# SSD stage: the mask is taken out of the matrix products, relu per head and one exponential over eight heads on ScalarE, inputs times step sizes as a product on VectorE

## The reference

```python
def ssd_chunked(xh, dt, A, Bm, Cm):
    x = (xh * dt[..., None]).reshape(...)
    a_cs = jnp.cumsum((dt * A).reshape(...), axis=2)
    seg = a_cs[:, :, :, None] - a_cs[:, :, None, :]
    decay = jnp.exp(jnp.where(causal, seg, -jnp.inf))
    cb = jnp.einsum('bclgn,bcsgn->bclsg', Cc, Bc)
    y_diag = jnp.einsum('bclsg,bclsgr,bcsgrp->bclgrp', cb, decay, x)
    decay_to_end = jnp.exp(a_cs[:, :, -1:] - a_cs)
    states = jnp.einsum('bclgn,bclgr,bclgrp->bcgrpn', Bc, decay_to_end, x)
    chunk_decay = jnp.exp(a_cs[:, :, -1])
    ...  # prev: the states before each chunk, from a scan over chunks
    y_off = jnp.einsum('bclgn,bcgrpn,bclgr->bclgrp', Cc, prev, jnp.exp(a_cs))
    return y_diag + y_off
```

## Time and profile before

| what | value |
|---|---|
| median of 3 runs | 1305.43 us (1304.57 to 1306.7) |
| profiled execution, its own time | 1318.41 us |
| its span | 1316.6 us |
| mean granted TensorE clock | 0.993 |
| TensorE busy, matmuls | 1268.5 us (96% of the span) |
| VectorE busy | 626.0 us (48%) |
| ScalarE busy | 386.7 us (29%) |
| GpSimd busy | 720.0 us (55%) |

### The profile page before, as it was taken

How to read it: one execution, slowest core, us unless ns; L and a number is a source line. 1 busy time by engine, 2 the same in 40 slices (tenths; PEclk the granted TensorE clock), 3 DMA queues, 4 the chain that set the end, 5 groups by cost and what they waited for, 6 DMA issues and landing times.

```text
span 1316.6 us, 19001 instructions
## 1 busy us (share of the span) xinstructions
PE 1268.5 (96%) x7442; PEld 911.3 (69%) x7442; DVE 626.0 (48%) x1035; ACT 386.7 (29%) x766; POOL 720.0 (55%) x752
## 2 busy tenths in 40 slices
PE   7999989999999999999999999999998989999997
PEld 7888768787788667888887887888887333333333
DVE  4252361448993583625854686633416322222225
ACT  5111272422333584112124644621113111111111
POOL 6677636576775302766774355665843555555430
PEclk9999999999999999999999999999999989999999
DMA  6622211432132200242222214832297599999965
GB/s 240 182 80 97 96 34 47 153 102 97 64 129 96 97 1 1 96 164 97 96 73 77 60 50 144 336 96 86 74 394 264 202 400 358 386 386 390 392 247 192
DMA packets 86845, 216.54 MB, mean 164 GB/s; under 512 B 24292, under 2 KB 33484, under 8 KB 73188
## 3 DMA queue, kind: packets, MB, share of 16 engines
q1 hardware_dynamic: 63132, 199.36, 41.2%
q0 software_dynamic: 14064, 8.45, 2.2%
q10 hardware_dynamic: 9560, 7.51, 1.9%
HBM read 252.98 MB, written 25.96 MB: 212 GB/s over the span
## 4 chain that ended last, share of the span: by engine, by line
PE 81%; DVE 7%; another core or an unknown queue 4%; ACT 2%; issue 2%; POOL 2%; DVEq 2%; DMA 0%; SPq 0%; POOLq 0%; ACTq 0%
PE ps L186 18%; PE ps L188 18%; PE ps L187 18%; PE ps L1217 10%; PE ps L1232 3%; PE ps L882 2%; POOL w_lo L1296 1%; PE ps L1095 1%; PE ps L1003 1%; PE ps L1208 1%; PE ps L1011 1%; PE ps L1087 1%; PE ps L1106 1%; DVE ps L2507 1%
## 5 line engine op out<-in xcount | busy, mean ns | idle before, releaser
L1293 POOL CAST w_hi<-stage 128x512 fp32r<-128x512 f32 (+1 forms) x280 | 179.4, 682 | 359.8 <-PE ps L188 350.0
L1296 POOL TENSOR_TENSOR w_lo<-stage,w_hi 128x512 fp32r<-128x512 f32 (+1 forms) x280 | 363.3, 1328 | 10.1
L186 PE MATMUL ps<-hi,w_hi 128*128 128x512 f32 (+1 forms) x608 | 236.9, 390 | 1.2 <-DVE lo L1890 0.6
L187 PE MATMUL ps<-hi,w_lo 128*128 128x512 f32 (+1 forms) x608 | 235.0, 386 | 0.0
L188 PE MATMUL ps<-lo,w_hi 128*128 128x512 f32 (+1 forms) x608 | 235.0, 386 | 0.0
L186 PE MATMUL ps<-w_hi,hi 128*128 128x512 f32 (+1 forms) x488 | 176.0, 361 | 1.5 <-POOL w_lo L1296 0.9
L187 PE MATMUL ps<-w_hi,lo 128*128 128x512 f32 (+1 forms) x488 | 174.7, 358 | 0.0
L188 PE MATMUL ps<-w_lo,hi 128*128 128x512 f32 (+1 forms) x488 | 174.7, 358 | 0.0
L1217 PE MATMUL ps<-w_gu,xT 128*64 128x512 f32 x736 | 166.0, 604 | 0.4 <-DVE xT L2526 0.4
L186 PEld LDWEIGHTS ps<-hi,w_hi 128*128 128x128 f32 x608 | 114.2, 188 | 27.7 <-issue 3.0
L188 PEld LDWEIGHTS ps<-lo,w_hi 128*128 128x128 f32 x608 | 114.2, 188 | 23.2
(11 more groups left out here) (489 smaller groups left out, 1763.5 us busy)
## 6 DMA issues: line engine op xcount, KB each, us to landing
stage<-w_in SPq DMA_DIRECT2D x84, 512.0 KB, 4.5
w_gu<-w_gate SPq DMA_DIRECT2D x32, 1024.0 KB, 10.0
w_gu<-w_up SPq DMA_DIRECT2D x32, 1024.0 KB, 11.9
w_dn<-w_down SPq DMA_DIRECT2D x32, 1024.0 KB, 14.4
stage<-w_out SPq DMA_DIRECT2D x16, 512.0 KB, 4.5
stage<-w_ssd_branch SPq DMA_DIRECT2D x16, 512.0 KB, 4.8
stage<-w_in SPq DMA_DIRECT2D x20, 256.0 KB, 3.1
stage<-w_attn_branch SPq DMA_DIRECT2D x8, 512.0 KB, 4.2
```

The lines of the kernel that those rows point to most:

```text
L186: pe.matmul(out, x[0], w[0], start=first, stop=False)
L187: pe.matmul(out, x[1], w[0], start=False, stop=False)
L1293: nc.gpsimd.tensor_copy(hi[:, b, k, 0:n], stage[:, b, k, 0:n])
L1296: last = nc.gpsimd.tensor_tensor(lo[:, b, k, 0:n], stage[:, b, k, 0:n], hi[:, b, k, 0:n].bitcast(F32), ALU.subtract)
```

## The change

The masks (L1066) go, with their constants, casts and loads. PSUM then holds the cumulated sum of the later token alone. Per head, ScalarE takes relu(sum of the earlier token - sum of the later one), which is zero where the later token comes first, and after eight heads one exponential of minus that, in place in `decay`. The triangle in `cb` removes what is then 1 there. dt is no longer in the exponent: VectorE multiplies the inputs with it (`xd`), TensorE's products read `xd` and wait for `xd_ready`, and `xe` is made from `xd`. The cap of `weighted` goes, so it is a plain product. `xe` shares its place with `yoff`, which takes one more drain. The waits for `acs_ready` (TensorE) and for `mT_saved` (VectorE) go too.

```diff
@@ SP
             sp.wait_ge(mT_half, 2)
-            sp.dma_start(block_of[:], d["c_block"]).then_inc(block_in, 16)
-            sp.dma_start(later[:], d["c_later"]).then_inc(block_in, 16)
             sp.dma_start(mT_dram, mT[:]).then_inc(mT_saved, 16)
@@ TensorE, spread
                 for b in range(4):
                     turns.bank(b, turns.k)
-                    rows = slice(64 * (b % 2), 64 * (b % 2 + 1))
-                    pe.matmul(ps[s][:, b, :].rearrange("p (h l) -> p h l", h=4), block_r[rows, :], bc(later_r[rows, :], 1, 4), start=True, stop=False)
...
-                                         acs_rows[rows, P * c:P * (c + 1)], start=False, stop=(j == 3))
+                                         acs_rows[rows, P * c:P * (c + 1)], start=True, stop=True)
...
-            pe.wait_ge(acs_ready, 1)
...
                 s = turns.take()
+                pe.wait_ge(xd_ready, c + 1)
...
-                        last = pe.matmul(ps[s][l, h // 8, HD * (h % 8):HD * (h % 8 + 1)], decay[:, h, l], xtok[:, c, HD * h:HD * (h + 1)],
+                        last = pe.matmul(ps[s][l, h // 8, HD * (h % 8):HD * (h % 8 + 1)], decay[:, h, l], xd[:, h, :],
@@ ScalarE
-                    A.wait_ge(dt_step, 3)
-                    A.activation(dt_log[:], dts[:, 2], ACT.Ln).then_inc(dt_act, 1)
...
-            A.activation(acs[:, 2], acs[:, 0], ACT.Exp, scale=-1.0)
+            A.activation(acs[:, 2], acs[:, 0], ACT.Exp)
...
-                        last = A.activation(decay[:, hh, :], ps[s][:, h // 4, P * (h % 4):P * (h % 4 + 1)], ACT.Exp,
-                                            bias=from_bias[:, c, hh:hh + 1])
+                        last = A.activation(decay[:, hh, :], ps[s][:, h // 4, P * (h % 4):P * (h % 4 + 1)], ACT.Relu,
+                                            scale=-1.0, bias=acs[:, 0, c, hh:hh + 1])
                         if h % 8 == 7:
-                            last.then_inc(e_ready, 1)
                             A.drain().then_inc(turn_free[s], 1)
+                            some = decay[:, hh - 7:hh + 1, :]
+                            A.activation(some, some, ACT.Exp, scale=-1.0).then_inc(e_ready, 1)
@@ VectorE
-            V.tensor_scalar(dts[:, 2], dts[:, 0], 1e-37, None, ALU.max)
...
-            V.tensor_scalar(acs[:, 0], sums[:, :, 0, :], -1.0, None, ALU.mult)
+            V.tensor_copy(acs[:, 0], sums[:, :, 0, :])
...
-            V.wait_ge(dt_act, 3)
-            V.tensor_tensor(from_bias[:], dt_log[:], acs[:, 0], ALU.add)
-            V.drain()
-            V.tensor_tensor(acs[:, 1], acs[:, 3], from_bias[:], ALU.add)
-            V.wait_ge(mT_saved, 16)
-            V.wait_ge(block_in, 32)
-            V.tensor_copy(later_r[:], later[:])
-            V.tensor_copy(block_r[:], block_of[:])
+            V.tensor_tensor(acs[:, 1], acs[:, 3], acs[:, 0], ALU.subtract)
...
-                    V.scalar_tensor_tensor(m, m, 3e38, bc(cb[:, g, :], 1, 8), ALU.min, ALU.mult).then_inc(m_ready, 1)
+                    V.tensor_tensor(m, m, bc(cb[:, g, :], 1, 8), ALU.mult).then_inc(m_ready, 1)
...
                 V.tensor_tensor(skip[:], heads(c), bc(d_skip[:], 2, HD), ALU.mult)
+                V.tensor_tensor(xd[:], heads(c), bc(dts[:, 0, c, :], 2, HD), ALU.mult).then_inc(xd_ready, 1)
...
                     V.tensor_tensor(skip[:], skip[:], yoff[:], ALU.add)
+                    V.drain()
                 if c < TT - 1:
-                    V.tensor_tensor(xe[:], heads(c), bc(acs[:, 1, c, :], 2, HD), ALU.mult).then_inc(xe_ready, 1)
+                    V.tensor_tensor(xe[:], xd[:], bc(acs[:, 1, c, :], 2, HD), ALU.mult).then_inc(xe_ready, 1)
```

More of the change, by code:

```diff
@@ L168, in consts @@
     c["c_quarter"] = (k // QUARTER)[:, None]
-    c["c_block"] = np.tile(k[None, :] // 2 == np.arange(64)[:, None], (2, 1))
-    c["c_later"] = np.tile(np.where(k[None, :] // 2 < np.arange(64)[:, None], NEG, 0.0), (2, 1))
     c["c_order"] = np.broadcast_to(np.arange(8, 0, -1), (P, 8))
@@ L308, in program @@
         mT = at("mT", 100, [P, KC, S])
-        skip, xe = at("skip", 0, [P, 32, HD]), at("xe", 8, [P, 32, HD])
-        yoff = at("yoff", 104, [P, 32, HD])
-        block_of, later = at("block_of", 8, [P, P]), at("later", 8.5, [P, P])
+        skip, xd = at("skip", 0, [P, 32, HD]), at("xd", 8, [P, 32, HD])
+        yoff = xe = at("yoff", 104, [P, 32, HD])
         xtok = at("xtok", 16, [P, TT, 2048])
@@ L325, in program @@
         acs = at("acs", 116, [P, 4, TT, 32])
-        dt_log, from_bias = at("dt_log", 113, [P, TT, 32]), at("from_bias", 113.5, [P, TT, 32])
-        later_r, block_r = at("later_r", 112, [P, P], F32R), at("block_r", 112.5, [P, P], F32R)
         sgb = at("sgb", 72, [P, KC, S])
@@ L427, in program @@
         mT_ready = sem("mT_ready")
-        block_in = sem("block_in")
+        xd_ready = sem("xd_ready")
         yal_ready = sem("yal_ready")
```

## The result

The changed kernel takes 1313.98 us (median of 4 runs, 1313.12 to 1315.36) against 1305.7 us for the kernel before beside it. The ratio is 1.0064, with a 95% interval of 1.0052 to 1.0077: slower by about 8.3 us. The direction is the one forecast; the size is nearly double the 4.4 us forecast. The profiled executions say the opposite of the runs if only their spans are compared (1311.2 us after, 1316.6 before), because the one taken of before was long in its last stage: 325.3 us from the router to the end, where the changed kernel's took 311.4. So the stage itself has to be read.

A forecast was written before the change was run, and what follows sets the result against it. Only what moves TensorE's instructions was held to count, with ScalarE pacing its waits. 4.47 us in blocks 1 to 3 less 0.08 in block 0 gave +4.4, so 1305.43 became 1309.9 us, range 1306.3 to 1314.0.

The forecast's parts named there:

- Step 1: TensorE's 32 masks go: first half 0.66 us earlier in blocks 1 to 3, second half saves 0.42; block 0's ScalarE start unmoved.
- rival A: ScalarE does not pace and the wide exponential hides, leaving only the masks' gain: -1.6 us, 1303.8; chance 0.15.
- rival D: New TensorE gaps of 1.2 and 0.3 us a block lower its clock in three z jobs: 1314.4 us; chance 0.03.
- Steps 2 and 3: ScalarE prices: eight relus cost 2.29 us like the exponentials they replace; each of 16 new wide exponentials adds 0.95.
- g: ScalarE's time for a group of eight heads, relus plus wide exponential: 3.24 us, range 3.22 to 3.46.
- Step 4: TensorE's z job waits for its third tile's bank, freed by ScalarE: +1.49 us a block, +4.47 in blocks 1 to 3.
- a margin of 0.8 us: Before the change, ScalarE frees the banks of the z job's third tile just 0.8 us ahead of TensorE.
- rival C: Each change between relu and exponential on ScalarE reloads the table at 1.28 us: about +30 us, 1335; chance 0.02.
- Step 5: Block 0's z job reads the first half's banks; its third tile could start at 728.46 against 728.54: -0.08 us.
- Steps 6 to 8: VectorE's added xd, the removed Ln, casts and loads, and GpSimd's later weight split: cost 0.
- Step 6: VectorE's xd costs 2.29 us a block but is hidden; chain behind the last group 9.1 us, cover left 1.5.
- B: VectorE becomes the bound, its three wide instructions after the last group 1 us slower each: 1312.9 us; chance 0.08.

## Why the prediction was half right

**What bounds the kernel**: right. Only TensorE's waits moved the time, and the stage's blocks add up to all of it.

**Step 1, the masks**: right in the gain, 0.42 us a block forecast and 0.32 to 0.44 measured in blocks 1 to 3, 1.65 in sum with block 0 against 1.6 forecast for rival A. The bulk of their time was cover for the wait on VectorE. The step did not say that it leaves a gap of 1.6 us on TensorE, and rival D did not count it.

**Steps 2 and 3, the prices**: right. The relu's pitch is the exponential's (747.01 to 749.27 for eight with their drain, 2.26 us), the wide exponential takes 1.06 us, g is 3.22. The run with the early load holds these terms without the load: its blocks 1 and 2 are 1.49 and 1.48 us longer than before, where 1.49 was forecast. The figures of the Trainium skill (ScalarE: Activation LUTs, What ACT_TABLE_LOAD costs) would have made g 3.30 and the block 1.67 by its estimate; the trace, with a g of 3.22, is with the rows.

**Step 4** failed, and it is the step that made the size wrong. It counted ScalarE's instructions from R on and took the table load to stay where it was, in idle time ahead of R; no step lists it. The sum lacked 3 x 1.28 = 3.84 us, the load behind the first eight relus in blocks 1 to 3. 4.4 + 3.8 is 8.2, against 8.3 measured; that it is so close is in part luck, since block 3 lost 0.2 us more than this and block 0 0.1 less. The two runs that moved the load, alone and in opposite directions, show it: 1.24 to 1.28 us in each of blocks 1 to 3 come back when it goes early, 1.5 us a block, with the small silu, are lost when it goes late in the kernel before. The step's other reading, a margin of 0.8 us that the change acts on, holds only for the third tile; the first had 0.04. This did not touch the sum, because with the new g the third tile decides.

What is instructive is that both facts needed stood in the text, under rival C. It asked whether every change of function loads a table, found that relu needs no load, and dismissed the matter. The same fact, that relu runs under whatever table is there (the Trainium skill, ScalarE: Activation LUTs, Table sets: the hidden batching unit; the trace agrees, relus at 747.01 run under silu's table), says that a relu does not call the load either. It passes the load on to the next exponential, and that one stood behind the wait.

**Step 5, block 0**: right, -0.18 against -0.08. There the load stays ahead, since the three small exponentials come first.

**Steps 6 to 8**: right. VectorE's, SP's and GpSimd's parts cost nothing in the changed kernel. Step 6's cover was real, and larger than priced: VectorE's chain behind the last group took 8.4 us (761.32 to 769.76) and not 9.1, and its wait ahead of the adds was 2.20 us in blocks 1 and 2, where 1.5 was forecast. With all relus first it was used up.

**Rivals**: A and B did not come about, nor C as it was stated. D did not show in the changed kernel, whose clock is 1.00 through the stage, but a fall of the clock behind a gap of TensorE does occur in this stage, in the traces of three other versions. Why in those and not in others is open.

## What to carry to other kernels

When a function on ScalarE is exchanged for one that needs no table of its own, look for the table load of the old one: here it moved to the next instruction that did need it, and with it behind the wait and the work that stood there. Look at the record of the load itself, and at the idle time around it, before and after. Where an engine frees buffers for a paced engine, do first the work that frees them and last the work that only others read; and price each pipeline's first block by itself. A product removed from a stretch in which TensorE waits anyway gave back little here (1.65 us for 7.4 us of records), and the gap that it left was followed by a lower clock in two traces.

## What the runs showed of the hardware

- A gap of 1.6 us between short products of 32 rows was followed by a granted clock of 0.50, for about 3 us, in block 2 of two traces (4.79 and 5.40 us for L1077, which takes 3.70); a gap of 1.40 us ahead of block 0's picks was followed by one in two traces as well (3.48 and 3.69 us for what takes 2.07). The changed kernel, with gaps of 1.6, 1.07 and 1.13 us in a block, had 1.00 there, and so had others with the same gaps. Six throw-away products in the gap cost next to nothing in the stage; the median with them was 1.8 and 2.0 us lower, on another chip.
- A table load was carried out ahead of the wait of the instruction that it belongs to: in the kernel before at 739.15, though the exponential could only start at 747.63. One exponential of one element per partition, 0.20 us, was enough to place it.
- A load with the wait already over cost its 1.28 us and no more: 1.24 to 1.28 us a block.
- With part of the arithmetic ahead of the router left out, the last stage was 24 and 6 us longer in two runs and unchanged in a third. TensorE's waits for the experts' weights grew in the first two; why is open. The total of such a run says nothing of the part left out until its last stage is compared.
